# Four edits to a fused two-block network on one Trainium2 core: products inside a layer norm's mean, modulation blocks moved behind the residual updates, a z buffer in PSUM, and the first norm's squares in places of their own

## Time and profile before

| | us |
|---|---|
| three runs | 1678.98, 1676.01, 1678.94 |
| their median | 1678.94 |
| the profiled execution | 1676.09 |
| its span, first to last instruction | 1674.3 |
| PE busy (matmuls) | 1634.5, 98% of the span |
| DVE busy | 812.1 |
| POOL busy | 727.0 |
| ACT busy | 577.9 |

### The profile page before, as it was taken

One profiled execution on the slowest core, in us unless ns is written; L12 is line 12 of the kernel. 1 busy time (PEld: TensorE's weight loads), 2 busy tenths in 40 slices (PEclk: granted clock), 3 DMA queues, 4 the chain that ended last, 5 costly groups with the idle time before them and its releaser, 6 DMA issues.

```text
span 1674.3 us, 21091 instructions
## 1 busy us (share of the span) xinstructions
PE 1634.5 (98%) x7286; PEld 1328.1 (79%) x7286; DVE 812.1 (49%) x1265; ACT 577.9 (35%) x790; POOL 727.0 (43%) x342
## 2 busy tenths in 40 slices
PE   7999999999999999999999999999999999999997
PEld 5785677878878888888878888888888888888886
DVE  6899788888575343433365161351525411111114
ACT  5424334443434322222243332333333432222233
POOL 4799224452344444444444243243424344444442
PEclk8999999999999999999999999999999999999999
DMA  9352266384475555554442222222212223222221
GB/s 375 121 194 76 76 205 241 115 305 147 169 268 192 200 199 189 185 199 170 167 170 88 77 93 92 75 76 86 88 63 89 81 95 101 99 89 100 92 75 60
DMA packets 65442, 233.71 MB, mean 140 GB/s; under 512 B 7264, under 2 KB 7264, under 8 KB 65120
## 3 DMA queue, kind: packets, MB, share of 16 engines
q1 hardware_dynamic: 65376, 232.82, 39.7%
HBM read 230.69 MB, written 2.10 MB: 139 GB/s over the span
## 4 chain that ended last, share of the span: by engine, by line
issue 54%; POOL 24%; PE 9%; DVE 6%; ACT 1%; DMA 1%; DVEq 1%; POOLq 1%; ACTq 0%
POOL w_lo L477 23%; PE bank L1494 2%; PE bank L1495 2%; PE bank L1496 2%; DVE mods_ring L1044 1%; DMA mods_ring<-w_mods_in 1%; DVE ps_stat L1166 1%; DVE ps_bc L1166 1%; DVEq L1189 1%; PE bank L1525 1%; PE bank L1529 1%; PE bank L1526 1%; DVE z_buf L1224 1%; PE ps_stat L1557 0%; DVE x L1090 0%
## 5 line engine op out<-in xcount | busy, mean ns | idle before, releaser
L477 POOL TENSOR_TENSOR w_lo<-w_raw,w_hi 128x1024 fp32r<-128x1024 f32 x268 | 644.8, 2411 | 894.9 <-ACT w_hi L561 879.7
L1494 PE MATMUL bank<-h_hi,w_hi 128*128 128x512 f32 x1240 | 485.1, 391 | 2.7 <-DVE h_lo L1121 2.6
L1496 PE MATMUL bank<-h_hi,w_lo 128*128 128x512 f32 x1240 | 482.8, 389 | 0.0
L1495 PE MATMUL bank<-h_lo,w_hi 128*128 128x512 f32 x1240 | 482.8, 389 | 0.0
L561 ACT ACTIVATE w_hi<-w_raw 128x1024 fp32r<-128x1024 f32 x264 | 277.8, 1052 | 261.0 <-PE bank L1496 254.8
L1494 PEld LDWEIGHTS bank<-h_hi,w_hi 128*128 128x128 f32 x1240 | 233.0, 188 | 52.7 <-issue 2.2
L1496 PEld LDWEIGHTS bank<-h_hi,w_lo 128*128 128x128 f32 x1240 | 232.9, 188 | 49.1
L1495 PEld LDWEIGHTS bank<-h_lo,w_hi 128*128 128x128 f32 x1240 | 233.0, 188 | 48.4 <-issue 0.5
L1494 PE MATMUL bank<-f_hi,w_hi 128*128 128x512 f32 x472 | 184.9, 392 | 6.9 <-POOL w_lo L477 5.3
L1495 PE MATMUL bank<-f_lo,w_hi 128*128 128x512 f32 x472 | 185.1, 392 | 0.0
L1496 PE MATMUL bank<-f_hi,w_lo 128*128 128x512 f32 x472 | 183.6, 389 | 0.0
(11 more groups left out here) (244 smaller groups left out, 1863.4 us busy)
## 6 DMA issues: line engine op xcount, KB each, us to landing
mods_ring<-w_mods_in SPq DMA_DIRECT2D x152, 512.0 KB, 6.0
w_raw<-ff_in_in SPq DMA_DIRECT2D x88, 512.0 KB, 3.4
w_raw<-ret_in SPq DMA_DIRECT2D x64, 512.0 KB, 3.4
w_raw<-ff_out_in SPq DMA_DIRECT2D x32, 512.0 KB, 3.5
w_raw<-cv_ab_in SPq DMA_DIRECT2D x16, 512.0 KB, 5.5
w_raw<-ff_tail_in SPq DMA_DIRECT2D x16, 384.0 KB, 3.0
w_raw<-cv_g_in SPq DMA_DIRECT2D x8, 512.0 KB, 3.5
w_raw<-cv_out_in SPq DMA_DIRECT2D x8, 512.0 KB, 3.5
```

Source lines behind the costliest of these rows:

```text
L477: pool.tensor_tensor(w_lo[:, s, :], w_raw[:, s, :], w_hi[:, s, :].bitcast(F32), ALU.subtract).then_inc(lo_done, 1)
L1494: pe.matmul(out, w_h, m_h, start=start, stop=False)
L1495: pe.matmul(out, w_h, m_l, start=False, stop=False)
L1496: return pe.matmul(out, w_l, m_h, start=False, stop=stop)
```

## The change

The first norm's squares go to eight places in `cv_g`, DVE adds them in pairs there, ACT no longer waits between them, and two of ACT's weight copies go ahead of the root and two ahead of the copy of `rb`. PE gets additional matmuls whose results are not used (eight of 128 columns before the broadcast of c, one of 512, and one of 384 behind each set of columns), and in the first projection takes w_lo by h_hi one chunk later. In the convolution's layer norm, nine products of the gate's last tile go ahead of the mean's chunk 6. In `out` on DVE the modulation blocks go behind each tile's update and square, in the numbers given by `blocks`, and `prepare` goes from tile 6 to tile 7. For `cv_out`, group 6 too goes into the loop, so that 16 blocks stand behind tiles 0 to 6; for `fr_out` 16 blocks behind tiles 0 to 3; for the first feed-forward network four blocks behind tile 0 and four behind tile 1. `pl_v` is cleared at its edges only. The z of the group products goes to two PSUM banks.

```diff
+EARLY_CHUNKS = 3
+        pool_z = (ps_bc, ps_stat)
@@ scalar: first norm
-                if c >= 2:
-                    act.wait_ge(x_sum, c // 2)
-                act.activation((sq, rb)[c % 2][:], x[:, c, :], ACT.Square).then_inc(sq_ready, 1)
+                act.activation(cv_g[:, c, :], x[:, c, :], ACT.Square).then_inc(sq_ready, 1)
...
             first_hi(0)
+            first_hi(1)
             std(ST["n0"], D)
-            first_hi(1)
-            act.wait_ge(bc_done, 1)
-            act.wait_ge(x_sum, DC // 2)
-            act.activation(rb[:], ps_bc[:], ACT.Copy).then_inc(rb_ready, 1)
             first_hi(2)
             first_hi(3)
+            act.wait_ge(bc_done, 1)
+            act.activation(rb[:], ps_bc[:], ACT.Copy).then_inc(rb_ready, 1)
@@ scalar: group products
-                hi(h_hi[:, j, :], j % 2)
+                act.activation(h_hi[:, j, :], pool_z[j % 2][:], ACT.Copy).then_inc(zh_ready, 1)
@@ vector: out
+                done = 0
                 for j in range(DC):
-                    if g is not None and halves and j < 2 * upto:
-                        sum_blocks(g + j // 2, (2 * (j % 2), 2 * (j % 2) + 1))
-                        if j % 2:
-                            end_mods(g + j // 2)
-                    if g is not None and not halves and j < upto:
-                        sum_mods(g + j)
-                    if stat is not None and ahead is None and j == DC - 2:
+                    if stat is not None and ahead is None and j == DC - 1:
                         prepare(int(stat[1]))
...
                         scaled_lo(*ahead, stat, due(j, first))
+                    for _ in range(blocks[j] if g is not None and j < len(blocks) else 0):
+                        sum_blocks(g + done // SLOTS, (done % SLOTS,))
+                        done += 1
+                        if done % SLOTS == 0:
+                            end_mods(g + done // SLOTS - 1)
@@ vector: calls
-            sum_mods(6)
-            v.memset(pl_v[:], 0.0).then_inc(win_step, 1)
-            out("cv_out", 0, "n1", g=7, upto=3, halves=True)
+            v.memset(pl_v[:, :, 0:PAD], 0.0)
+            v.memset(pl_v[:, :, PAD + T:], 0.0).then_inc(win_step, 1)
+            out("cv_out", 0, "n1", g=6, blocks=(2, 2, 2, 3, 3, 2, 2))
-            out("pl_out", 1, "n2", g=17, upto=2, halves=True, ahead=(f_hi, f_lo), shift=float(T))
+            out("pl_out", 1, "n2", g=17, blocks=(2, 2, 2, 2), ahead=(f_hi, f_lo), shift=float(T))
-            out("fr_out", 2, "n3", g=19, upto=4)
+            out("fr_out", 2, "n3", g=19, blocks=(SLOTS,) * 4)
@@ tensor: first norm
+            for _ in range(BUSY["constants"]):
+                pe.matmul(bank[0][:, 0:P], ones[:], ident[:], start=True, stop=True)
+            pe.wait_ge(vec_in, 16)
             spread_c(0)
+            keep_busy(1, bank[0])
             for p in range(DC // 2):
                 pe.wait_ge(x_sum, p + 1)
...
+                keep_busy(1, bank[0], 3 * P)
@@ tensor: mean of the layer norm
+                if c == 6:
+                    unit_ready("cv_g", 2 * SLOTS - 1)
+                    bank_ready("cv_g", 2 * SLOTS - 1)
+                    for k in range(EARLY_CHUNKS):
+                        tile(SLOTS - 1, k, h_hi, h_lo, DC)
```

More of the change, by code:

```diff
@@ L69 @@
 ACT_TAPS = 13
-BUSY = {"std": 1, "last square": 1, "norm": 2, "conv": 6, "squares": 3, "layer norm": 4, "first norm": 4}
+BUSY = {"std": 1, "last square": 1, "norm": 2, "conv": 6, "squares": 3, "layer norm": 4, "first norm": 4, "constants": 8}
 SHIFT = [3 * DC * n for n in range(7)]
@@ L1068, in lo, with out @@
                 v.tensor_tensor(dst, z_buf[:, q, :], hi, ALU.subtract).then_inc(zl_ready, 1)
-            def out(name, n, stat, per_unit=1, g=None, upto=2, ahead=None, first=0, shift=None, halves=False):
+            def out(name, n, stat, per_unit=1, g=None, blocks=(SLOTS, SLOTS), ahead=None, first=0, shift=None):
+                done = 0
                 for j in range(DC):
-                    if g is not None and halves and j < 2 * upto:
-                        sum_blocks(g + j // 2, (2 * (j % 2), 2 * (j % 2) + 1))
-                        if j % 2:
-                            end_mods(g + j // 2)
-                    if g is not None and not halves and j < upto:
-                        sum_mods(g + j)
-                    if stat is not None and ahead is None and j == DC - 2:
+                    if stat is not None and ahead is None and j == DC - 1:
                         prepare(int(stat[1]))
@@ L1130, in _ @@
                 v.wait_ge(sq_ready, 2 * p + 2)
-                if p >= 2:
-                    v.wait_ge(x_used, p - 1)
-                v.tensor_tensor((ssum, diag)[p % 2][:], sq[:], rb[:], ALU.add).then_inc(x_sum, 1)
+                v.tensor_tensor(cv_g[:, 2 * p, :], cv_g[:, 2 * p, :], cv_g[:, 2 * p + 1, :],
+                                ALU.add).then_inc(x_sum, 1)
             inverse(ST["n0"])
@@ L1611, in _ @@
             pe.wait_ge(const_ready, 1)
+            for _ in range(BUSY["constants"]):
+                pe.matmul(bank[0][:, 0:P], ones[:], ident[:], start=True, stop=True)
+            pe.wait_ge(vec_in, 16)
             spread_c(0)
+            keep_busy(1, bank[0])
             for p in range(DC // 2):
                 pe.wait_ge(x_sum, p + 1)
-                last = p == DC // 2 - 1
-                columns((ssum, diag)[p % 2], p == 0, last).then_inc(stat_done if last else x_used, 1)
-            pe.wait_ge(vec_in, 16)
-            keep_busy(BUSY["std"], bank[0])
+                last = columns(cv_g[:, 2 * p, :], p == 0, p == DC // 2 - 1)
+                if p == DC // 2 - 1:
+                    last.then_inc(stat_done, 1)
+                keep_busy(1, bank[0], 3 * P)
             spread(ST["n0"])
             keep_busy(BUSY["first norm"], bank[0])
-            four_tiles("cv_ab", 0, h_hi, h_lo, ready=h_part(0), upto=DC - 2)
+            part = lambda k: slice(k * P, (k + 1) * P)
+            hi_ready, lo_ready = h_part(0)
+            for k in range(DC - 1):
+                if k < DC - 2:
+                    hi_ready(k)
+                    for s in range(SLOTS):
+                        if k == 0:
+                            pe.wait_ge(hi_done, s + 1)
+                        pe.matmul(bank[s][:], w_hi[:, s, part(k)], h_hi[:, k, :], start=k == 0, stop=False)
+                    lo_ready(k)
+                    for s in range(SLOTS):
+                        pe.matmul(bank[s][:], w_hi[:, s, part(k)], h_lo[:, k, :], start=False, stop=False)
+                if k:
+                    for s in range(SLOTS):
+                        if k == 1:
+                            unit_ready("cv_ab", s)
+                        pe.matmul(bank[s][:], w_lo[:, s, part(k - 1)], h_hi[:, k - 1, :], start=False, stop=False)
+            for s in range(SLOTS):
+                for k in (DC - 2, DC - 1):
+                    if s == 0:
+                        hi_ready(k)
+                        lo_ready(k)
+                    last = tile(s, k, h_hi, h_lo, DC)
+                last.then_inc(unit_used, 1)
             with pe.Fori(1, 4) as i:
@@ L1661, in _ @@
                     pe.wait_ge(centered, DC)
-                for k in range(DC):
+                for k in range(EARLY_CHUNKS if s == SLOTS - 1 else 0, DC):
                     last = tile(s, k, h_hi, h_lo, DC)
```

8 lines of the change are left out of this document (5 added, 3 removed).

## The result

| | before | after |
|---|---|---|
| median | 1677.47 us (4 runs) | 1686.76 us (4 runs) |
| profiled execution | 1676.09 | 1686.65 |
| its span | 1674.3 | 1684.9 |
| PE busy | 1634.5 | 1642.7 |

The medians differ by 9.3 us (ratio 1.0055); the ratio on record is 1.0061, 95% interval 1.0045 to 1.0077. The change makes the kernel slower, as forecast. The forecast was 11.2 us more, and 1690 us in all; between the two profiled executions it was 10.6 us.

The account below looks back on a forecast made before the run. PE was taken as the bound, busy in nearly every slice. Terms -3.1, -1.3, +6.7, -2.0, +4.9, +3.0 and +3.0 sum to +11.2: 1687.3 profiled, plus 2.85 for the median, forecast 1690 us; 8-in-10 range 1678 to 1698.

Parts of the forecast that it names:

- The first norm: First norm: weight copies and rb done before the second block product, so DVE's first chunk starts earlier; -3.1 us.
- the added matmuls cost nothing: First norm: PE's added filler matmuls cost nothing while PE waits for DVE there.
- The root could even be 1 us late: First norm: the root could be 1 us late before the copy of rb passed 19.15, leaving -3.1.
- The mean: Mean, before chunk 6: nine products fill PE's standstill, so the slow passes at 1.2 GHz go; -1.3 us.
- cv_out: cv_out: later block sums delay pl_v's load, ACT's refill, the square of tile 5 and the last updates; +6.7 us.
- Group products: Group products: with z in PSUM the subtraction always takes 0.68 us and w_lo comes earlier; -2.0 us.
- fr_out: fr_out: 16 blocks behind the first updates delay update 4, and prepare waits for POOL before the last update; +4.9 us.
- First network: First feed-forward network, part 2: update 2 comes later behind the second group, and prepare adds 0.3; +3.0 us.
- Clock: PE slowed after longer standstills behind cv_out and fr_out: 1.7 for fr_out, 1.3 for the rest; +3.0 us.
- A: cv_out: SP's load chain does not bite and updates follow PE, giving 1668 us; chance 0.11.
- B: Same places but mildly: load in 3.4 us, no POOL wait in fr_out, clock +1; +1.7, 1681 us; chance 0.18.
- C: First norm: PE at 1.2 GHz with fillers makes root and DVE's first chunk later, about 2: 1695 us; chance 0.08.

Follow-up runs that it names:

- e4: Kernel after with PE's added matmuls without use, the mean's nine early gate products and z in PSUM all undone: 1693.29 us, ratio 1.009.
- e7: Kernel before with only the moved modulation blocks and prepare at tile 7, pl_v still cleared whole: 1694.62 us, ratio 1.0114.
- e2: Kernel after with the first four units of pl_v loaded ahead of group 9 instead of behind it: 1684.46 us, ratio 1.0047.
- e5: Kernel after with one block of each of cv_out's tiles 0 to 6 moved between update and addition of the square: 1686.20 us, ratio 1.0057.
- e9: Kernel after with the four units of pl_v and four blocks of group 9 taken in turn in the load queue: 1681.25 us, ratio 1.0028.
- e11: Kernel after with blocks partly ahead of updates, partly around square additions, prepare earlier, and pl_v units and group 9 blocks loaded in turn: 1657.88 us, ratio 0.9892.
- e10: Kernel after with prepare of fr_out alone at tile 4 instead of tile 7: 1685.52 us, ratio 1.0053.

## Why the prediction held, point by point

The sum was +11.2 and the profiles differ by 10.6. The forecast of 1690 was 3.2 us above the measured median, and most of that is no term of the sum: I had added 2.85 us because the median before lay that far above its profiled execution, but a fourth run brought that median to 1677.47, and after the change the median lies 0.1 above its profile. Part of the agreement of the sum is luck, since errors of opposite sign met in it: 0.7 us more gain by an early first load and 1.5 more in the group products, against 1.0 in `fr_out` for a wait that I had not costed.

- **The first norm, -3.1.** Right: 3.06 us at equal landing, and 0.65 to 0.7 more by chance of the load (first block product at 16.09 instead of 16.79). The statement that the added matmuls cost nothing was right, but they are half of the gain (e4), which I had not seen. "The root could even be 1 us late" was wrong; it left out the spread behind the root, and in e4 a root at 16.23 puts DVE's first chunk at 20.84: from root to `rb` it is 3.62 us without the added matmuls (16.23 to 19.85) and 2.06 with them (14.31 to 16.37).
- **The mean, -1.3.** Right in this trace (-1.7). e7 shows what it rests on: the standstill alone costs nothing that can be seen; the fall of the clock behind it costs the 1.7, and it doesn't come every time.
- **cv_out, +6.7.** The mechanism is right in each link: load, refill, square, update. e2, e5 and e9 move the time at which the load is asked for, and the end follows. In the times of day of the trace after, the shift of 5.5 us taken off, my terms read 243.3 for the third block's summing (msum of group 8: 243.4), 243.6 for the issue (243.83), 250.2 for the landing (249.83) and 259.9 for the last update (259.50). Against before the last update is 6.3 later (forecast 6.7); the other 1.3 of the stage's 7.6 come behind it, in a norm that PE works at half clock (a row of eight sums of squares takes 1.86 us, before 0.95 and 1.05).
- **Group products, -2.0.** Right in mechanism, mis-sized: the 3.4 us at half clock disappeared whole, where I took a quarter of their 1.7 back. Measured were -3.5, beyond my bound of -3.3, but only 2.8 of them belong to z; 0.75 come before that, from the place at which DVE, between waits for blocks' loads, frees the first bank, which I had not looked at.
- **fr_out, +4.9 and 1.7 of clock.** From the last addition to the last update, with `prepare` waiting for POOL: forecast 3.5 us, took 3.2. Update 4 was forecast at 491.2 and came at 491.04, but the stage had begun 1.44 us earlier: the blocks waited for a load (1.02 at 474.69), which I had not costed. So the last update is 5.9 later than before, measured in the stage, where I had 4.9; 1.8 more come behind it, at half clock.
- **First network, +3.0.** The second wait for w_lo was there, 2.40 us before 865.03, forecast 2.7. The 0.3 for `prepare` was not paid in this trace (DVE waited for PE behind it), and the 3.4 us at half clock belong to the next term. In e2, where the same stage ran wholly at full clock, it is at +3.4.
- **Clock, +3.0.** This term is right as a sum, and its parts are argued rather than measured alone. What came behind the last updates is 1.3 in `cv_out` and 1.8 in `fr_out`. In the network the last update itself was already 4.2 late and nothing came behind it; against e2 the half clock cost 0.9 there. The group products gave back 1.3 more than I took, if all of the 1.7 is counted. Together this is 2.7. `cv_out` had 17.1 us at half clock, and before only 3.4.
- **Rivals.** A is out: its point (group 8 summed before 244.5, shifted to 239.0, or the square not behind the refill) is not met. In e11, where no square waits for the refill, the updates do follow PE: 1657.9, better than A's 1668. B's milder load did not come: 6.0 us; its terms also add up to +2.7, not +1.7, which would have been 1682. C is out, since the first chunk came earlier.

## What to carry to other kernels

Work moved behind the critical step must be followed to the queues that wait for it: here the summing of a block released a DMA, that DMA stood ahead of another load, and ACT waited for this load ahead of the square that DVE needed. The remedy was not to undo the move but to take the two loads in turn and to place one piece of filler work where DVE waits for ACT anyway. Tiny instructions with two SBUF operands belong where the other engine on that memory stands still.

## What the runs showed of the hardware

- The first 512 KB load of `pl_v` took 6.0 us in `cv_out` after (243.83 to 249.83), and 5.6 (e4) to 7.1 us (e5) in the twelve traces in which ACT waited for it, from SP's issue on; the median of the 88 loads of `ff_in_in` in the earlier trace rows is 3.4. The estimate from the Trainium skill (DMA: Bandwidth & Descriptors, Anatomy of one DMA), 3.2 us, fits that median and not this load. In its 6.0 us the DMA engines were busy to 0.94; in e9, at 0.79, it took 6.9.
- `prepare`'s two instructions, at most 128x16, took 0.17 each in e10 and 1.01 and 2.26 beside POOL; a copy of 128x4 took 0.16 to 1.57 after. DVE's z subtraction with one operand in PSUM always took 0.68, with both in SBUF up to 2.03. The Trainium skill (SBUF — State Buffer, Who interferes with whom) says that an instruction of VectorE with two SBUF inputs contends with a GpSimd instruction that reads SBUF, and that one with a single SBUF input does not, outside the modes that use both port pairs, which copies can enter: the rows agree, those of the small copy too. Its other rule, that VectorE is slower from PSUM (VectorE: DVE Perf Modes, The TRN2 errata), they don't show: with both operands in SBUF and POOL standing still the subtraction took 0.68 as well.
- PE's clock after the same standstill of 1.8 to 2.0 us fell in two kernels (before and e4, where the four passes took 3.21 and 3.20 us) and did not in e7 (1.98 us). What decides it, these runs don't show.
- The first loads land within 1.4 us of each other from profile to profile (first block product at 15.92 to 17.32), and later times shift with it. Measured from that product, the first unit is used after 28.91 to 29.0 us in nine of the kernels.
